# Splitting each run of eight back groups around the last unit of a round in the first feed-forward

## The chip, the cores and the metric

One NeuronCore of a Trainium2 chip runs the whole program. The metric is the time of one execution on the device in microseconds (us); the kernel before takes 2517.07 us, the median of three runs (2516.57 to 2520.61).

## What is computed

Two transformer blocks follow each other on 1024 tokens of width 1024, in float32. The change lies in the feed-forward of the first:

```python
h = rmsnorm(x, norm2_w)
u = causal_dwconv(h @ w_up, ffn_conv_w)          # 3 taps, 2 * 2816 columns
gate, up = u[..., :D_FF], u[..., D_FF:]          # D_FF = 2816 = 22 * 128
x = x + (jax.nn.silu(gate) * up) @ w_down
```

Ahead of it stand a mixer (a gated delta rule and a dilated attention) and its output projection; behind it the second block, with a gated and a convolving branch and a feed-forward of its own. The second block's first part (in2, with a convolution of 31 taps, and out2) is laid into the second half of the first feed-forward.

## The kernel before

**Arithmetic.** A product in float32 is made of three in a rounded format: each weight tile `w` is split into a high part `wh` (ScalarE, line 960) and a low part `wl = w - wh` (VectorE, line 1335), each activation into `hh`/`hl` or `fh`/`fl`, and TensorE adds wh*h, wh*hl and wl*h. Activations lie with channels on partitions and tokens along the free side, and tokens are taken in two halves of 512 (a = 0 and 1).

**Units.** A weight tile of 128 x 1024 numbers (512 KB) is a unit, numbered in order of use. A `gate` or `up` unit is 24 matmuls of 512 columns (lines 2140 to 2142) into one of the banks 0 to 2. Two `down` units are used together as a run of eight groups (lines 2157 to 2159), one group of six matmuls for each 128 rows of x; groups take turns in banks 3, 4 and 5, so that group t needs the bank of group t-3, freed when VectorE has added it into x (line 1638). A matmul starts every 0.227 us, so that a unit is 5.44 us and a group 1.36.

**A round** (`ffn1(a, p)` and `down(1, a, p - 1)`) makes the activations 2p and 2p+1 and projects those of the round before back to 1024 channels: gate A, up A, gate B, up B, then a run of eight groups. There are 11 rounds for each half; the first round of a = 0 has no run, and the run of the last activations of a = 0 stands in the first round of a = 1. After a unit ScalarE evacuates it (1168 and 1170 or 1172, 1175), VectorE makes two passes of the short convolution (1643, 1649). ScalarE takes silu of the gate (1196), VectorE multiplies (`fin`, 1654), ScalarE rounds to fh (1202), VectorE makes fl (`low`, 1658). `fin` and `low` of a pair are put in front of the next gate unit's stage (at a round's end, of the next round's gate A).

**Weights.** There are two raw buffers (unit k uses k % 2) and four slots of wh and wl (k % 4). SyncE's queue loads unit k (line 858) when the low part of unit k-2 is done, or its high part alone where k-2 is "kept". ScalarE's split of unit k waits for that load, and for TensorE to be done with unit k-4. The gate, up and down units of a = 1 are kept, 66 of them: their low parts are those of a = 0, which GpSimd's queue has stored (935), and SyncE's queue brings them back into wl (868) when TensorE is done with unit k-4. The order is load(k), then the bringing back of k-1, on one queue.

**Order.** The class `Dense` writes one list of stages, and every engine and queue walks it in that order, leaving out what is not its own. So an instruction that waits holds back all that is behind it on its engine. A split is put in front of each unit (`prep(at + 3)`), behind group 2 of a run and behind the run. The planner keeps two clocks, `matmul_us` and `vector_us` (5.44 for a unit, 1.36 for a group, 1.28 for VectorE's part of a split, 0.66 for most other passes), and `background` puts norms, gating and the taps of the long convolution in front of a unit or group as long as VectorE's clock plus the item (and, for norms, a reserve of 1.5) does not pass TensorE's. A norm is the items `ax` (VectorE's scaling, 1677, then ScalarE's high part, 1178) and `al` (VectorE's low part, 1611), in the order ax ax al al.

Of the kernel before, what the change touches and what calls it, by code (L numbers as in the profile page):

```python
# [25 lines left out]
KT = D // P  # L26
# [5 lines left out]
FF1 = 2816 // P  # L32
# [11 lines left out]
N_A, N_B, F_A, N_A2, F_B, N_B2, O_A, O_B = 0, 1, 2, 4, 5, 7, 8, 9  # L44
# [44 lines left out]
class Dense:  # L89
# [32 lines left out]

        return self.counts[signal, stage]

    def prep(self, k):


        if k < U_DENSE:
            self.put("high" if k in self.kept else "prep", k)

# [38 lines left out]

    def single(self, stage, late=()):  # L170

        self.prep(self.at + 3)
        for item in late:
            self.put(*item)
        self.matmul_us = max(self.matmul_us, self.vector_us - UNIT_US) + UNIT_US
        self.background(self.matmul_us)
        n = len(self.singles)
        self.tile[stage], self.bank[stage] = self.at, (n % 3, self.singles[n - 3] if n >= 3 else None)
        self.singles.append(stage)
        self.at += 1  # L180
        self.put(*stage)

    def down(self, f, a, p, stats=None):

        self.tile["down", f, a, p] = self.at
        for t in range(KT):
            stage = ("group", f, a, p, t)
            self.matmul_us = max(self.matmul_us, self.vector_us - 2 * GROUP_US) + GROUP_US
            if stats is None:
                self.background(self.matmul_us)  # L190
            n = len(self.groups)
            self.bank[stage] = 3 + n % 3, (self.groups[n - 3] if n >= 3 else None)
            self.groups.append(stage)
            self.put(*stage)
            if t == 2:
                self.prep(self.at + 3)
            if stats is not None:
                for item in self.square(stats, t):
                    self.put(*item)
        if stats is not None:  # L200
            self.put("acc", stats, KT - 2)
            self.put("acc", stats, KT - 1)
        self.at += 2
        self.prep(self.at + 2)

    def square(self, r, k):

# [29 lines left out]
            late = self.square(r, n)  # L237
        return late + [("acc", r, KT - 2), ("acc", r, KT - 1)]

    def ffn1(self, a, p, late=()):  # L240

        for j in (2 * p, 2 * p + 1):
            self.single(("gate", a, j), late)
            self.put("two", a, j)
            self.single(("up", a, j), [("silu", a, j)])
            self.put("two", a, j + FF1)
            self.act[1, a, j] = len(self.act)
            late = [("fin", a, j), ("low", 1, a, j)]
        return late

# [29 lines left out]

    def block_one(self):

        self.prep(self.at + 2)
        late = self.out(1, 0, N_A)
        self.norms += self.factor(N_A) + self.halves(N_A)
        late = self.out(1, 1, N_B, late)
        self.finish(self.norms)
        self.norms += self.factor(N_B) + self.halves(N_B)
        self.reserve = 1.5
        for a in range(2):  # L290
            for p in range(FF1 // 2):
                if (a, p) == (0, 2):
                    self.gating += [("gturn",), "|", "|", ("gbias",)]
                late = self.ffn1(a, p, late)
                if (a, p) == (1, 0):
                    self.reserve = 0.0
                    self.down(1, 0, FF1 // 2 - 1, F_A)
                    self.norms += self.factor(F_A) + self.in_place(F_A) + self.factor(F_A + 1) + self.halves(F_A + 1)
                elif p:
                    self.down(1, a, p - 1)  # L300
                if (a, p) == (1, IN2_AFTER[0]):
                    self.finish(self.norms)
                    late = self.in2(0, late)
                elif (a, p) == (1, OUT2_AFTER[0]):
                    self.drain()
                    late = self.out(2, 0, N_A2, late)
                    self.norms += self.factor(N_A2) + self.halves(N_A2)
        self.finish(self.norms)
        self.block_two(late)

    def block_two(self, late):

        for a in range(2):
            for p in range(FF2 // 2):
                late = self.ffn2(a, p, late)
                if (a, p) == (0, 0):
                    self.down(1, 1, FF1 // 2 - 1, F_B)
                    self.norms += self.factor(F_B) + self.in_place(F_B) + self.factor(F_B + 1) + self.halves(F_B + 1)
                elif (a, p) == (1, 0):
                    self.down(2, 0, FF2 // 2 - 1, O_A)  # L320
                    self.norms += ["|", ("fcols", 0), "|", ("finv", 0)]
                    for t in range(4):
                        self.norms += ["|", ("fturn", 0, t)]
                elif p:
                    if (a, p) == (1, FF2 // 2 - 1):
                        for item in late:
                            self.put(*item)
                    self.down(2, a, p - 1)
                if (a, p) == (0, IN2_AFTER[1]):
                    self.finish(self.norms)  # L330
                    late = self.in2(1, late)
                elif (a, p) == (0, OUT2_AFTER[1]):
                    self.drain()
                    late = self.out(2, 1, N_B2, late)
                    self.norms += self.factor(N_B2) + self.halves(N_B2)
            self.finish(self.norms)
        self.down(2, 1, FF2 // 2 - 1, O_B)
        for item in [("fcols", 1), ("finv", 1)] + [("fturn", 1, t) for t in range(4)]:
            self.put(*item)
# [205 lines left out]
def program(nc, a, out):  # L545

    ctx = ExitStack()
    with ctx:
# [190 lines left out]
        def cols(w, c):  # L739

            return w.rearrange("(k p) n -> p k n", p=P)[:, :, bass.ds(c, P)]

        def rows(w, r):
            return w[bass.ds(r, P), :]
# [15 lines left out]
        dense = Dense(kept)  # L760
# [5 lines left out]
        def _(sp):  # L766
            def load(k, src, m=0, i=0, down=False):

                if k >= 2:
                    sp.wait_ge(s["w_lo"], k - 1 + m * i)  # L770
                dst = raw[:, k % 2] if down else raw[:, k % 2].rearrange("p (k n) -> p k n", k=KT)
                sp.dma_start(dst, src).then_inc(w_loaded[k % 2], 16)
# [94 lines left out]
                        sp.wait_ge(st_free[k % 4], 112 + 16 * sent_before(k))  # L867
                    sp.dma_start(wl[:, k % 4].bitcast(F32), wl_s[:, kept[k]]).then_inc(tile_moved[k % 4], 16)

            for stage in dense.order:  # L870
                if stage[0] == "out":
                    k, n = unit_of[stage], stage[3]
                    if k >= U_OUT1 + 4:
                        load(k, cols(w_out if stage[1] == 1 else w_out2, n * P))
                elif stage[0] == "gate":
                    load(unit_of[stage], cols(w_up, stage[2] * P))
                elif stage[0] == "up":
                    load(unit_of[stage], cols(w_up, (FF1 + stage[2]) * P))
                elif stage[0] == "ffn2":
                    load(unit_of[stage], cols(w_ff1, stage[2] * P))  # L880
                elif stage[0] == "u":
                    load(unit_of[stage], cols(w_in2, stage[2] * P))
                elif stage[0] == "v":
                    load(unit_of[stage], cols(w_in2, (GH + stage[2]) * P))
                elif stage[0] == "val":
                    load(unit_of[stage], cols(w_in2, (2 * GH + stage[2]) * P))
                elif stage[0] == "sig":
                    load(unit_of[stage], cols(w_in2, (3 * GH + stage[2]) * P))
                elif stage[0] == "group" and stage[4] == 0:
                    k, p = unit_of[("down",) + stage[1:4]], stage[3]  # L890
                    for m in range(2):
                        load(k + m, rows(w_down if stage[1] == 1 else w_ff2, (2 * p + m) * P), down=True)
# [59 lines left out]
        def _(act):  # L952
# [45 lines left out]
            square(1)  # L998
            square(2)
            prep(0, 0)  # L1000
            act.wait_ge(s["par_ready"], 1)
            for j in range(4):
                high(j)
            prep(1, 1)
            high(4)
            high(5)
# [21 lines left out]
            for n in range(12):  # L1028
                prep(n + 2, (n + 2) % 4)
                act.wait_ge(s["scaled"], n + 1)  # L1030
                if n >= 4:
                    act.wait_ge(st_free[n % 4], 16 * (n // 4))
                A(st[:, n % 4], acc(n % 2 if n != 2 else 2), ACT.Copy, scale=(0.125 if n < 4 else 1.0)).then_inc(s["st_written"], 1)
# [1242 lines left out]
```

## Time and profile before

| | us |
|---|---|
| median of three runs | 2517.07 |
| lowest, highest | 2516.57, 2520.61 |
| profiled execution | 2516.36 |
| its span (first to last instruction) | 2514.6 |
| TensorE busy in the span | 2465.0 (98%) |
| VectorE busy | 1510.5 (60%) |
| ScalarE busy | 1098.6 (44%) |
| granted TensorE clock | 0.996 of full |

Busy time of TensorE counts the overlapping records of matmuls once. The 16 engines of the DMA moved 304.36 MB, 121 GB/s on average. All durations below come from the profiled execution. Times in it run from the start of the span.

### The profile page before, as it was taken

To read this page: it belongs to the slowest core of one execution; us is meant where nothing else is said; L and a number is where in the kernel's file an instruction comes from. 1 tells how busy PE (TensorE), PEld (TensorE's weight loads), DVE (VectorE), ACT (ScalarE), POOL (GpSimd) and SP (SyncE) were. 2 spreads that over 40 slices of the span, in tenths; PEclk is the share of its full clock that TensorE was granted. 3 is DMA by queue.
4 is the path that set the end of the run, shared out by engine and by line. 5 is a ranking of instruction groups with operands and counts; after the bars stand their busy time and mean duration, and the time that the engine had idled before them with its cause. 6 is when DMAs were issued, how large, how long until landed. Compare 5 with 4: busy or idle time off the path is not lost.

```text
span 2514.6 us, 35248 instructions
## 1 busy us (share of the span) xinstructions
PE 2465.0 (98%) x13947; PEld 2025.6 (81%) x13947; DVE 1510.5 (60%) x2483; ACT 1098.6 (44%) x1783; POOL 55.2 (2%) x110
## 2 busy tenths in 40 slices
PE   7999999999999999999999999999999999999998
PEld 5888777787788888888888788787888888888887
DVE  4234546666366766656669844565888646655555
ACT  4123247776545444446444453444333433433332
POOL 0000000000000011000000000000000000000000
PEclk9999999999999999999999999999999999999999
DMA  6322330110445565565435564423323332333332
GB/s 212 104 84 84 121 118 19 61 61 19 124 122 173 193 201 188 198 209 178 141 93 185 158 193 132 153 84 93 93 84 92 101 99 86 117 106 96 98 88 82
DMA packets 318646, 304.36 MB, mean 121 GB/s; under 512 B 10271, under 2 KB 277908, under 8 KB 318356
## 3 DMA queue, kind: packets, MB, share of 16 engines
q1 hardware_dynamic: 301956, 241.30, 32.4%
q0 software_dynamic: 14400, 56.11, 5.5%
q10 hardware_dynamic: 2128, 4.72, 0.5%
q8 instruction: 111, 1.82, 0.3%
q14 instruction: 51, 0.42, 0.1%
HBM read 244.41 MB, written 57.67 MB: 120 GB/s over the span
## 4 chain that ended last, share of the span: by engine, by line
PE 88%; DVE 6%; ACT 2%; issue 2%; DMA 1%; SPq 0%; DVEq 0%; ACTq 0%
PE PS L2140 15%; PE PS L2142 14%; PE PS L2141 14%; PE PS L1794 11%; PE PS L2157 7%; PE PS L2159 7%; PE PS L2158 7%; PE PS L1965 3%; PE PS L2099 1%; PE PS L1951 1%; PE PS L2075 1%; PE PS L2087 1%; DVE cg L1741 1%; DVE x L1638 1%; DMA raw<-in_w_ff 1%
## 5 line engine op out<-in xcount | busy, mean ns | idle before, releaser
L2140 PE MATMUL PS<-hh,wh 128*128 128x512 f32 x1728 | 677.8, 392 | 2.4 <-DVE hl L1611 1.6
L2142 PE MATMUL PS<-hh,wl 128*128 128x512 f32 x1728 | 673.5, 390 | 0.0
L2141 PE MATMUL PS<-hl,wh 128*128 128x512 f32 x1728 | 673.1, 390 | 0.0
L960 ACT ACTIVATE wh<-raw 128x1024 fp32r<-128x1024 f32 x352 | 366.7, 1055 | 482.5 <-PE PS L2159 343.1
L1335 DVE TENSOR_TENSOR wl<-raw,wh 128x1024 fp32r<-128x1024 f32 x286 | 346.1, 1222 | 280.1 <-ACT wh L960 279.9
L1638 DVE TENSOR_TENSOR x<-x,PS 128x512 f32<-128x512 f32 x432 | 292.6, 683 | 167.3 <-PE PS L2159 166.0
L2140 PEld LDWEIGHTS PS<-hh,wh 128*128 128x128 f32 x1728 | 325.0, 188 | 71.9 <-DVE hl L1611 3.3
L2142 PEld LDWEIGHTS PS<-hh,wl 128*128 128x128 f32 x1728 | 324.8, 188 | 68.0
L2141 PEld LDWEIGHTS PS<-hl,wh 128*128 128x128 f32 x1728 | 325.1, 188 | 66.8 <-issue 0.5
L2157 PE MATMUL PS<-fh,wh 128*128 128x512 f32 x856 | 339.1, 396 | 9.0 <-DVE x L1638 8.9
L2159 PE MATMUL PS<-fh,wl 128*128 128x512 f32 x856 | 334.2, 390 | 0.0
L2158 PE MATMUL PS<-fl,wh 128*128 128x512 f32 x856 | 333.8, 390 | 0.0
L2157 PEld LDWEIGHTS PS<-fh,wh 128*128 128x128 f32 x856 | 161.1, 188 | 47.6 <-DVE x L1638 13.5
L2158 PEld LDWEIGHTS PS<-fl,wh 128*128 128x128 f32 x856 | 161.2, 188 | 34.4 <-issue 1.7
L2159 PEld LDWEIGHTS PS<-fh,wl 128*128 128x128 f32 x856 | 161.0, 188 | 33.9
L1741 DVE SCALAR_TENSOR_TENSOR cg<-cg,par 128x512 f32<-128x512 f32 x240 | 169.7, 745 | 1.3
L1794 PE MATMUL PS<-hh,wh 128*128 128x512 f32 x416 | 129.4, 392 | 0.0
L1794 PE MATMUL PS<-hl,wh 128*128 128x512 f32 x416 | 128.3, 390 | 0.0
L1794 PE MATMUL PS<-hh,wl 128*128 128x512 f32 x416 | 128.1, 389 | 0.0
L1643 DVE SCALAR_TENSOR_TENSOR uc<-ubuf,par,uc 128x512 f32<-128x512 f32 x44 | 33.1, 751 | 107.9 <-ACT uc L1175 107.8
L1168 ACT ACTIVATE ubuf<-PS 128x512 f32<-128x512 f32 x88 | 52.5, 597 | 102.5 <-PE PS L2142 102.4
L1658 DVE TENSOR_TENSOR fl<-uc,fh 128x512 fp32r<-128x512 f32 x107 | 73.5, 687 | 36.7 <-ACT fh L1202 36.7
(302 smaller groups left out, 2567.6 us busy)
## 6 DMA issues: line engine op xcount, KB each, us to landing
raw<-in_w_ff SPq DMA_DIRECT2D x128, 512.0 KB, 4.0
raw<-in_w_up SPq DMA_DIRECT2D x88, 512.0 KB, 4.3
wl_s<-wl POOLq DMA_DIRECT2D x66, 512.0 KB, 5.4
wl<-wl_s SPq DMA_DIRECT2D x66, 512.0 KB, 3.5
raw<-in_w_in SPq DMA_DIRECT2D x59, 512.0 KB, 3.9
raw<-in_w_down SPq DMA_DIRECT2D x44, 512.0 KB, 5.5
raw<-in_w_out SPq DMA_DIRECT2D x32, 512.0 KB, 3.9
qkvz_s<-st POOLq DMA_DIRECT2D x16, 512.0 KB, 2.9
```

The source lines that it names most:

```text
L960: A(whs(slot), raw[:, k % 2], ACT.Copy).then_inc(s["w_hi"], 1)
L1335: TTo(wls(slot), raw[:, k % 2], whs(slot).bitcast(F32), ALU.subtract).then_inc(s["w_lo"], 1)
L1638: TTo(x[:, t, span(a_)], x[:, t, span(a_)], PS[:, bank, :], ALU.add).then_inc(s["x_done"], 1)
L1741: STT(c, cg[:, 2 + q, i:i + HALF], w, c, ALU.mult, ALU.add).then_inc(s["c_tap"], 1)
L1794: last = mm(acc(bank)[:, t * HALF:(t + 1) * HALF], w(slot)[:, cut], h[:, kk, t * HALF:(t + 1) * HALF], start=kk == order[0] and n == 0, st ...
L1965: last = mm(dst(q, h), left(q, h), right(q, h), start=True, stop=True)
L2140: mm(bank, wh[:, k % 4, cut], hh[:, kk, span(a_)], start=kk == 0, stop=False)
L2141: mm(bank, wh[:, k % 4, cut], hl[:, kk, span(a_)], start=False, stop=False)
L2142: last = mm(bank, wl[:, k % 4, cut], hh[:, kk, span(a_)], start=False, stop=kk == KT - 1)
L2157: mm(bank, wh[:, (k + m) % 4, cut], act_tile(True, f), start=m == 0, stop=False)
L2158: mm(bank, wh[:, (k + m) % 4, cut], act_tile(False, f), start=False, stop=False)
L2159: last = mm(bank, wl[:, (k + m) % 4, cut], act_tile(True, f), start=False, stop=m == 1)
```

## The change

In each round that has a run, the fourth unit (up B) is issued between groups 3 and 4 of the run. The four groups ahead of it take the down units' weights before up B is used, but up B keeps the lower unit number: its weights are loaded first, and SyncE's queue now walks a list sorted by unit number. The splits are counted by one running number. One still stands in front of gate A, up A and gate B, none in front of up B; one is put behind group 2, one behind group 6, and one behind the run. Background items may be put in front of each group and of up B as before. The second feed-forward is untouched.

```diff
-    def down(self, f, a, p, stats=None):
-
-        self.tile["down", f, a, p] = self.at
+    def down(self, f, a, p, stats=None, between=None):
+
+        d = self.at + (1 if between else 0)
+        self.tile["down", f, a, p] = d
...
-            if t == 2:
-                self.prep(self.at + 3)
+            if t == 2 or t == 6 and between:
+                self.split()
...
+            if between and t == KT // 2 - 1:
+                self.inner = True
+                between()
+                self.inner = None
...
-        self.at += 2
-        self.prep(self.at + 2)
+        self.at = d + 2
+        self.split()
```

```diff
     def single(self, stage, late=()):
-        self.prep(self.at + 3)
+        if self.split_next <= self.at + 3 and self.inner is None:
+            self.split()
```

```diff
-    def ffn1(self, a, p, late=()):
+    def ffn1(self, a, p, late=(), back=None):
         for j in (2 * p, 2 * p + 1):
+            self.act[1, a, j] = len(self.act)
             self.single(("gate", a, j), late)
             self.put("two", a, j)
-            self.single(("up", a, j), [("silu", a, j)])
-            self.put("two", a, j + FF1)
-            self.act[1, a, j] = len(self.act)
+
+            def up(j=j):
+                self.single(("up", a, j), [("silu", a, j)])
+                self.put("two", a, j + FF1)
+
+            if back and j % 2:
+                self.down(*back, between=up)
+            else:
+                up()
```

```diff
+        self.loads = [("group",) + stage[1:] + (0,) if stage[0] == "down" else stage
+                      for stage, _ in sorted(self.tile.items(), key=lambda item: item[1])]
...
-            for stage in dense.order:
+            for stage in dense.loads:
```

`split()` takes the next number from `split_next` and puts the same stage as `prep(k)` did.

## Rows read from the trace of the kernel before

**Rows 1.** The profile's page: TensorE's busy time, shares of the chain

```profile
PE 2465.0 (98%) x13947; PEld 2025.6 (81%) x13947; DVE 1510.5 (60%) x2483; ACT 1098.6 (44%) x1783; POOL 55.2 (2%) x110
...
PE 88%; DVE 6%; ACT 2%; issue 2%; DMA 1%; SPq 0%; DVEq 0%; ACTq 0%
```

**Rows 2.** Busy time by stretch: stretch, its us, then each engine, clock, DMA

```profile
756.00:1106.00 350.00, 350.00 (x1554) 289.77 (x1553) 229.22 (x296) 152.11 (x252) 32.42 (x61) 1.00 0.57 191
1106.00:1632.00 526.00, 520.49 (x2357) 428.94 (x2356) 335.43 (x493) 249.14 (x385) 1.35 (x3) 1.00 0.50 157
```

**Rows 3.** TensorE's waits from 1106 to 1632: total us, times, longest

```profile
PE PS L2157 <- DVE x L1638: 2.9, 3, 1.7
PE PS L2169 <- ACT cs L1304: 1.5, 2, 0.9
PE PS L2140 <- DVE hl L1611: 1.1, 1, 1.1
```

**Rows 4.** Time line of TensorE: start us, us, engine, line, what

```profile
964.70 0.39 PE L2157 MATMUL PS<-fh,wh 128*128 128x512 f32 x1
...
975.58 0.39 PE L2140 MATMUL PS<-hh,wh 128*128 128x512 f32 x1
...
997.34 0.39 PE L2157 MATMUL PS<-fh,wh 128*128 128x512 f32 x1
```

**Rows 5.** Time line of VectorE in the run from 964.70

```profile
969.58 1.22 DVE L1335 TENSOR_TENSOR wl<-raw,wh 128x1024 fp32r<-128x1024 f32 x1
```

**Rows 6.** Time line of ScalarE in the round from 975.58

```profile
975.84 2.01 ACT L960 ACTIVATE wh<-raw 128x1024 fp32r<-128x1024 f32 x2 [8.75 <-PE PS L2159]
...
981.22 0.60 ACT L1168 ACTIVATE ubuf<-PS 128x512 f32<-128x512 f32 x1 [0.59 <-PE PS L2142]
...
984.13 0.63 ACT L1196 ACTIVATE gc<-gc 128x512 f32<-128x512 f32 x1 [0.32 <-DVE gc L1649]
986.66 0.60 ACT L1168 ACTIVATE ubuf<-PS 128x512 f32<-128x512 f32 x1 [1.90 <-PE PS L2142]
...
991.30 0.63 ACT L1202 ACTIVATE fh<-uc 128x512 fp32r<-128x512 f32 x1 [2.46 <-DVE uc L1654]
992.10 0.60 ACT L1168 ACTIVATE ubuf<-PS 128x512 f32<-128x512 f32 x1 [0.16 <-PE PS L2142]
...
997.54 0.60 ACT L1168 ACTIVATE ubuf<-PS 128x512 f32<-128x512 f32 x1 [1.89 <-PE PS L2142]
```

**Rows 7.** Time line of VectorE in the same round

```profile
977.00 2.36 DVE L1335 TENSOR_TENSOR wl<-raw,wh 128x1024 fp32r<-128x1024 f32 x2 [0.53 <-ACT wh L960]
979.28 0.68 DVE L1654 TENSOR_TENSOR uc<-gc,uc 128x512 f32<-128x512 f32 x1
...
989.45 1.22 DVE L1335 TENSOR_TENSOR wl<-raw,wh 128x1024 fp32r<-128x1024 f32 x1
...
1000.33 1.98 DVE L1638 TENSOR_TENSOR x<-x,PS 128x512 f32<-128x512 f32 x3
```

**Rows 8.** Time line of SyncE's queue: the load behind rows 5

```profile
970.83 0.37 SPq L858 DMA_DIRECT2D raw<-in_w_up  x1
```

**Rows 9.** DMA issues, us to landing: from 970.5; the second of two, from 979.3

```profile
raw<-in_w_up SPq DMA_DIRECT2D x1, 512.0 KB, 4.3
...
raw<-in_w_down SPq DMA_DIRECT2D x1, 512.0 KB, 5.8
```

**Rows 10.** Time line of TensorE: the two long waits for adds into x

```profile
1168.44 0.50 PE L2157 MATMUL PS<-fh,wh 128*128 128x512 f32 x1 [1.67 <-DVE x L1638]
...
1621.26 0.50 PE L2157 MATMUL PS<-fh,wh 128*128 128x512 f32 x1 [1.04 <-DVE x L1638]
```

**Rows 11.** Line 868 from 1106 to 1632, all 64 transfers

```profile
DMA to landing us min/median/max: 3.2/3.5/6.8
```

**Rows 12.** Time line of ScalarE in a round with two ax

```profile
850.66 0.60 ACT L1168 ACTIVATE ubuf<-PS 128x512 f32<-128x512 f32 x1 [0.59 <-PE PS L2142]
...
856.57 0.58 ACT L1168 ACTIVATE ubuf<-PS 128x512 f32<-128x512 f32 x1
```

More of the change, by code:

```diff
@@ L123, in count, with split @@
         return self.counts[signal, stage]
-    def prep(self, k):
+    def split(self):
+        k, self.split_next = self.split_next, self.split_next + 1
         if k < U_DENSE:
@@ L281, in block_one @@
     def block_one(self):
-        self.prep(self.at + 2)
+        self.split_next, self.inner = self.at + 2, None
+        self.split()
         late = self.out(1, 0, N_A)
@@ L293, in block_one @@
                     self.gating += [("gturn",), "|", "|", ("gbias",)]
-                late = self.ffn1(a, p, late)
+                back = (1, 0, FF1 // 2 - 1, F_A) if (a, p) == (1, 0) else (1, a, p - 1) if p else None
                 if (a, p) == (1, 0):
                     self.reserve = 0.0
-                    self.down(1, 0, FF1 // 2 - 1, F_A)
+                late = self.ffn1(a, p, late, back)
+                if (a, p) == (1, 0):
                     self.norms += self.factor(F_A) + self.in_place(F_A) + self.factor(F_A + 1) + self.halves(F_A + 1)
-                elif p:
-                    self.down(1, a, p - 1)
                 if (a, p) == (1, IN2_AFTER[0]):
```

## The prediction

> **What bounds the kernel now.** I read the page's head first. TensorE is busy for 98% of the span and holds 88% of the chain that ended last [rows 1], so only time in which TensorE stands still, or new matmuls, can move the end. The change adds no matmul. Next the view by stretches, cut where the second half of the sequence begins: from 756 to 1106 us TensorE is busy for 350.00 of 350.00 us; from 1106 to 1632 us for 520.49 of 526.00 [rows 2]. The eleven rounds of the first feed-forward on tokens 0 to 511 lie in the first stretch, those on tokens 512 to 1023 in the second. The waits of TensorE in the second are 2.9 us on VectorE's adds into x, 1.5 on ScalarE's cs and 1.1 on hl, together 5.5 us [rows 3]. In the first there are none. That is the ceiling: a pure reordering cannot win more than 5.5 us (0.22%) here, and in the first half it can only lose. About 0.2% (5 us) is what a measurement of this kernel can tell from no change.
>
> Then the time lines of one undisturbed round, from its gate unit at 975.58 to group 0 at 997.34, a run before it from 964.70 [rows 4]. Call 975.58 "zero" of a round: gate A at 0, up A at 5.44, gate B at 10.88, up B at 16.32, groups 21.76 to 32.64, and the next round's gate A at 32.64. Beside it stand VectorE, ScalarE and the loads of the same round [rows 5 to 9]. What the reader is to see: both engines wait for TensorE in each unit, but in a fixed order, so one instruction that waits for a load holds all behind it.
>
> **Part 1, the groups.** Groups 0 to 3 move from 21.76 to 16.32; up B moves to 21.76; groups 4 to 7 stay at 27.20. Group 3 needs the bank of group 0. VectorE adds group 0 only after both passes over the unit before it: ScalarE begins that unit's evacuation at 997.54, VectorE's first add starts at 1000.33 [rows 6, 7], and lasts 0.68, so 3.47 us from evacuation to free bank. Group 3 starts 4.08 us after the unit's end and the evacuation 0.20 after it: 0.4 us of slack. It is now needed after gate B. If the evacuation of gate B is late by more than 0.4 us, group 3 waits for the excess; the wait of 1.67 us at 1168.44 [rows 10], which only such an add ended, shows this very thing, with a first matmul of 0.50 instead of 0.39. I add 0.1 for that.
>
> **Part 2, the weights of the pair of down units.** The second one's slot is freed by up A (10.88) and is now needed at 16.32 instead of 21.76. In the first half VectorE ends that split at 989.45+1.22 = 990.67, which is 15.09 [rows 7]: 1.2 us to spare. In the second half its low part comes by a transfer, issued when gate B starts; over all 64 of the second stretch such a one lands in 3.5 us at the median, 6.8 at the longest [rows 11]. Against 5.44 this holds as a rule, so I cost it nothing, and at most 1.4 us once or twice.
>
> **Part 3, the split that moves.** This is the step that costs. Six splits a round stay, but their places change: the one that stood in front of up B goes behind group 2, and the one behind group 2 goes behind group 6. Name the latter's unit n+7 (n is gate A's number). Unit n+9, the next up B, shares its raw buffer, so the queue of SyncE loads n+9 only when n+7's low part is done. In the trace that low part runs from 969.58 to 970.80 [rows 5] and ends 6.10 us after the run began (964.70); the load is issued at 970.83 and lands 4.3 us later [rows 8, 9]: 0.4 us before the next gate A at 975.58. Moved behind group 6, the chain of the second half-run has the same shape, but starts from up B's end at -5.44: low part done at +0.66, load issued at +0.69, landed at +5.0 to +5.1. The instruction that waits for it, the high part of n+9, stands on ScalarE in front of "fin" and gate A's evacuation; on VectorE its low part stands in front of the product of "fin".
>
> From rows, steady round, first half: high part of n+9 from 5.05; its low part 1.16 later (977.00 less 975.84) for 1.22, done at 7.43; product 0.68, done at 8.03; fh 0.63, done at 8.70; gate A's evacuation at 8.6 (neighbours overlap by 0.1) instead of 5.64 (981.22): 3.0 late. From there to the end of silu is 3.54 (984.13+0.63 less 981.22): up A's evacuation at 12.1, due at 11.08 (986.66): 1.0 late. From there 4.01 to the end of the low part of Part 2: 16.1, needed at 16.32, so it just holds. And 5.27 less 0.1 to the end of fh: gate B's evacuation at 17.3 instead of 16.52, 0.8 late. Less the slack of 0.4, plus 0.1: group 3 waits 0.5 us a round. Up B then lets both engines recover, and the next round loses it again, for the chain starts at up B's end.
>
> Who pays: rounds 2 to 10 of the first half (nine; the first run is in round 1). In the second half most splits have no low part on VectorE and loads go out once the high part is done, which ScalarE does right after up B's evacuation: nothing. Rounds 4 to 10: 7 times 0.5 = 3.5 us. Rounds 2 and 3 carry the norm of the other half as well. By the planner's costs the middle of the run takes four norm items in front of up B (it holds 23.0 of 27.2 us then), so in front of up A stand two "al" and the gate mask in round 2, two "ax" in round 3. Round 2: two "al" of about 0.7 and the mask of about as much (operations of 128x512 on VectorE, as the product at 979.28, 0.68 [rows 7]) behind the low part that ends at 12.6 make up A's first pass 1.1 later: 0.5+1.1 = 1.6. Round 3: with two ax, from gate A's evacuation (850.66) to up A's (856.57) take 5.91 [rows 12], so 8.6+5.9 = 14.5, 3.4 late; less 0.6 of slack along the way, plus 0.1: 2.9. Sum of the first half: 3.5+1.6+2.9 = 8.0 us. Its ends: 0, if some cover that I do not see takes up the 3 us (in the trace gate A's evacuation is never this late, so no row excludes it); and 16, if the loads land 0.9 us later (the second of two loads issued within 1.1 us of each other took 5.8 [rows 9]): 7 times 1.4, and 2.5 and 3.8.
>
> A weighing of the measured load: the row says 4.3 us for 512 KB. The Trainium skill, "DMA: Bandwidth & Descriptors", section "Anatomy of one DMA", gives a fixed 2.0 us and then bytes over 436 GB/s, fitted for DMAs that GpSimd issues; for this load an estimate by that page is 3.2 us. By it gate A's evacuation would be only 1.9 us late, silu would end before up A, steady rounds would lose nothing, and the first half some 2.5 us. The row decides; what the page would have is the second rival's condition. [...]
>
> **Part 4, the second half.** Of the 5.5 us of waits, 2.9 are in runs: one at group 3 with sums beside it (1.67), one at group 6 behind a split (1.04) [rows 10], and one of the rest. Two bursts of four give VectorE 5.44 us of room between them, so a wait at group 6 goes; one at group 3 behind a unit stays likely. The cs and hl waits lie where the planner drops them and may move. Bounds: -5.5, all gone, to +3, three new ones of the size of the 1.04. I take -1.5, half of the 2.9.
>
> **Sum.** Profiled execution: 2516.36 (span 2514.6 and 1.8 around it) + 8.0 - 1.5 = 2522.9. The median of the three runs is 0.7 above it: about 2523.5.
>
> **The rivals.** (A) The cover holds: something in front of the late split gives way and steady rounds lose nothing. For: the slack missed is only 0.4 us a round, the size of one overlap that I read off. Then the first half costs 0 to 4, less 1.5: 2517.5. (B) Faster: the late load costs nothing and the runs of the second half wait no more. Place: the bank waits in front of groups 3 and 6. Price: up to -5.5, so 2511.6. It decides if the load lands within about 3.3 us of its issue, so that gate A's evacuation is under 2 us late, and if cs and hl waits go too. Against: in the first half no row has such a load, and cs and hl are not touched by the split run. (C) The load lands later still, because the pair's next load and two stores of low parts follow at its heels: 5.8 instead of 4.3 [rows 9]. Then gate A is 4.5 late, up A 2.5, the down unit's low part ends at 17.6, and each steady round loses 2.0: 7 times 2.0 + 3.1 + 4.4 - 1.5 = 20 us, 2537; about 2530 if every second load is hit.
>
> **How the numbers follow.** Forecast 0.56 (2519 to 2528), A 0.24, B 0.08, C 0.12. Slower by over 0.2% (above 2522.1): most of the forecast and all of C, 0.60. Within: the forecast's low end and A, 0.33. Faster: B's far end, 0.07. Range: A's low end to C's half case, 2515 to 2531.
>
> **What would show it.** In the first half new waits of TensorE at group 3 on an add into x, nine of them, about 0.5 us each and larger in rounds 2 and 3; ScalarE's splits released by a load into raw (in_w_up) instead of by TensorE; gate A's evacuation 8.6 instead of 5.6 us into a round. If the first half stays at 350 of 350 us busy, Part 3 is wrong. If waits stand at group 0 on the split or on the landing, Part 2 was under-priced. If the second half's waits on x grow, Part 4 has the wrong sign.

## The result, and the profile after

The changed kernel takes 2539.61 us, median of three runs (2536.53 to 2539.79); the kernel before 2517.07. The ratio is 1.0081, interval 1.0061 to 1.0100: 20 us slower (the two medians alone are 22.5 apart). The forecast was slower by 6.5 us, 2523.5, with 2531 as the far end. The sign was right, and the first half of the sequence paid about what was forecast. The size was three times too small, because the second half, which was forecast to win 1.5 us, lost more than the first.

The line numbers of the changed kernel are 16 higher from the splits on: 976 is ScalarE's high part, 1351 VectorE's low part, 1184 to 1191 the evacuation, 1654 the add into x, 874 the load, 2156 to 2158 a unit, 2173 to 2175 a group. In the kernels of the experiments they stand 1 below to 8 above these (980 in e3 is 976 here). The page's head and its chain, as in [rows 1]:

```profile
PE 2474.1 (98%) x13947; PEld 2028.7 (80%) x13947; DVE 1505.8 (59%) x2483; ACT 1096.1 (43%) x1783; POOL 55.4 (2%) x110
...
PE 77%; DVE 10%; ACT 5%; issue 4%; DMA 3%; SPq 0%; DVEq 0%; ACTq 0%
```

TensorE is still busy for 98% of the span. It is the chain that tells: TensorE held 88% of it, now 77%, and VectorE, ScalarE and the DMA have what it lost. Busy time by stretch, as in [rows 2], cut at the same places of the program:

```profile
759.00:1116.00 357.00, 352.82 (x1552) 288.37 (x1552) 226.13 (x296) 149.51 (x251) 32.52 (x61) 1.00 0.57 186
1116.00:1652.00 536.00, 523.30 (x2355) 430.76 (x2354) 332.57 (x492) 248.65 (x384) 1.35 (x3) 0.99 0.49 153
```

The first half has lost its full 350 of 350: 4.2 us idle. The second has 12.7 us idle where it had 5.5, and a clock of 0.99. TensorE's waits of the second half (1120 to 1650), to be held against [rows 3]:

```profile
PE PS L2185 <- ACT cs L1320: 4.2, 2, 3.4
PE PS L2173 <- ACT wh L976: 2.9, 1, 2.9
PE PS L2173 <- DVE x L1654: 2.7, 2, 2.4
PE PS L2156 <- DVE hl L1627: 1.6, 1, 1.6
PE PS L2197 <- DVE small L1686: 0.3, 1, 0.3
```

When the starts of the same units are laid side by side (TensorE's time line, counted in units), the 20.1 us between the two spans fall apart as follows, each line rounded. An idle sum misses part of this. The wait of 0.24 us shown below belongs to a round that lost 0.57: neighbouring matmuls overlap (0.39 long, 0.227 apart), a wait breaks the overlap, and the first matmul behind it takes 0.50. Two longer waits also had a slow clock behind them (last section).

```
                                        us over before
ahead of the first feed-forward               2.5   (same program; 0.6 in a later execution)
tokens 0 to 511, rounds 2 and 3               4.0   (round 2 1.0, round 3 3.0)
                 rounds 4 to 10               3.7   (0.48 to 0.59 each)
                 round 1                     -0.3
tokens 512 to 1023, round 1 (its run)        -1.5
                 round 3                     +5.2
                 rounds 4, 5, 6        +1.9 +4.4 +0.4
                 round 10, and the unit behind it   -1.4 +1.5
```

**The first half as the prediction had it.** ScalarE in the round whose gate unit begins at 983.28, to be held against [rows 6] (start, length, instruction, what ended the wait before it):

```profile
983.54 1.06 ACT L976 ACTIVATE wh<-raw 128x1024 fp32r<-128x1024 f32 x1 [3.31 <-PE PS L2175]
988.42 1.06 ACT L976 ACTIVATE wh<-raw 128x1024 fp32r<-128x1024 f32 x1 [3.82 <-DMA raw<-in_w_up]
991.45 0.63 ACT L1218 ACTIVATE fh<-uc 128x512 fp32r<-128x512 f32 x1 [1.97 <-DVE uc L1670]
991.99 0.58 ACT L1184 ACTIVATE ubuf<-PS 128x512 f32<-128x512 f32 x1
...
995.42 0.58 ACT L1184 ACTIVATE ubuf<-PS 128x512 f32<-128x512 f32 x1
...
1000.59 0.58 ACT L1184 ACTIVATE ubuf<-PS 128x512 f32<-128x512 f32 x1
```

SyncE's queue in the same round, to be held against [rows 8]:

```profile
983.97 0.37 SPq L874 DMA_DIRECT2D raw<-in_w_up  x1
```

TensorE's wait at group 3 of that round:

```profile
1004.11 0.50 PE L2173 MATMUL PS<-fh,wh 128*128 128x512 f32 x1 [0.24 <-DVE x L1654]
```

And VectorE ahead of it, with the low part and the adds into x:

```profile
998.20 1.22 DVE L1351 TENSOR_TENSOR wl<-raw,wh 128x1024 fp32r<-128x1024 f32 x1
...
1003.37 1.88 DVE L1654 TENSOR_TENSOR x<-x,PS 128x512 f32<-128x512 f32 x3
```

The reader is to see one load, issued 0.69 us into the round, and a split that waits 3.82 us for it; fh and the evacuation of gate A follow on its heels, at 8.71 us into the round.

Rounds 2 and 3 pay in another place. TensorE's waits of the first half (756 to 1120), then, from round 3, whose gate unit begins at 848.14, VectorE's low part and the wait of TensorE that it ends:

```profile
PE PS L2173 <- DVE wl L1351: 2.5, 2, 2.2
PE PS L2173 <- DVE x L1654: 1.7, 8, 0.2
...
865.49 1.22 DVE L1351 TENSOR_TENSOR wl<-raw,wh 128x1024 fp32r<-128x1024 f32 x1
866.81 0.47 PE L2173 MATMUL PS<-fh,wh 128*128 128x512 f32 x1 [2.18 <-DVE wl L1351]
```

The eight waits on an add into x are those of group 3 in rounds 3 to 10. The two on wl stand at group 0 of rounds 2 (0.34) and 3 (2.18): the low part of the second down unit is done 18.6 us into round 3, and group 0 needs it at 16.3.

**The second half as it did not.** ScalarE at the end of round 2 and in round 3, whose gate unit begins at 1218.2:

```profile
1216.26 0.63 ACT L1194 ACTIVATE hh<-hn 128x512 fp32r<-128x512 f32 x1 [1.35 <-DVE hn L1693]
1217.53 0.63 ACT L1194 ACTIVATE hh<-hn 128x512 fp32r<-128x512 f32 x1 [0.63 <-DVE hn L1693]
1218.06 1.99 ACT L976 ACTIVATE wh<-raw 128x1024 fp32r<-128x1024 f32 x2
1222.93 1.06 ACT L976 ACTIVATE wh<-raw 128x1024 fp32r<-128x1024 f32 x1 [2.88 <-DMA raw<-in_w_up]
...
1226.53 1.30 ACT L1194 ACTIVATE hh<-hn 128x512 fp32r<-128x512 f32 x2 [2.02 <-DVE hn L1693]
1227.73 0.58 ACT L1184 ACTIVATE ubuf<-PS 128x512 f32<-128x512 f32 x1
...
1235.24 0.58 ACT L1184 ACTIVATE ubuf<-PS 128x512 f32<-128x512 f32 x1
...
1236.38 1.05 ACT L976 ACTIVATE wh<-raw 128x1024 fp32r<-128x1024 f32 x1
```

SyncE's queue there:

```profile
1219.13 0.38 SPq L874 DMA_DIRECT2D raw<-in_w_up  x1
```

The split of n+7 ought to follow up B's evacuation, 5 us before the round. It starts at 1218.06, because two copies of the norm stand ahead of it and each waits for VectorE. So the load goes out 0.9 us into the round, the split of n+9 waits for it, the copies behind it wait in turn, up A's evacuation is 6 us late, and the high part of the second down unit (1236.38) ends at 1237.43, when TensorE has been idle since 1234.7. TensorE's time line there:

```profile
1237.64 0.77 PE L2173 MATMUL PS<-fh,wh 128*128 128x512 f32 x1 [2.93 <-ACT wh L976]
...
1240.34 0.51 PE L2173 MATMUL PS<-fh,wh 128*128 128x512 f32 x1
```

And the stretches of the wait and just behind it. The granted clock is the first of the last three numbers, the DMA's share and its GB/s follow:

```profile
1234.70:1237.60 2.90, 0.01 (x1) 0.00 (x0) 0.97 (x2) 2.73 (x5) 0.00 (x0) 0.92 0.01 3
1237.60:1240.30 2.70, 2.66 (x6) 2.15 (x7) 1.90 (x4) 1.33 (x4) 0.00 (x0) 0.50 0.52 149
```

In round 5 it is the taps. The copies of the convolution's norm (1328, 1194) hold the split of n+7 until 1384.38, the load is issued at 1385.44, and VectorE, whose fl stands ahead of five taps, waits for the high part behind it:

```profile
1386.97 0.69 DVE L1670 TENSOR_TENSOR uc<-gc,uc 128x512 f32<-128x512 f32 x1
1391.02 0.69 DVE L1674 TENSOR_TENSOR fl<-uc,fh 128x512 fp32r<-128x512 f32 x1 [3.36 <-ACT fh L1218]
```

VectorE's 3.4 us of standing still are not made good, since the planner has filled it up to TensorE's clock, and TensorE pays them 19 us later, in front of the norm's sums, where the kernel before waits 0.65:

```profile
1409.90 1.05 PE L2185 MATMUL PS<-ones,cs 128*128 128x1 f32 x8 [3.42 <-ACT cs L1320]
```

### The profile page after: what moved, and what is told of

It reads as the page before. It is cut to its first block, busy times and chain, and to the rows that moved or that the text cites. A ratio compares the mean times of both kernels' runs of the same rounds, so it can differ in the third digit from the quotient of the medians.

```text
span 2534.7 us, 35248 instructions
## 1 busy us (share of the span) xinstructions
PE 2474.1 (98%) x13947; PEld 2028.7 (80%) x13947; DVE 1505.8 (59%) x2483; ACT 1096.1 (43%) x1783; POOL 55.4 (2%) x110
## 4 chain that ended last, share of the span: by engine, by line
PE 77%; DVE 10%; ACT 5%; issue 4%; DMA 3%; SPq 0%; DVEq 0%; ACTq 0%
PE PS L2156 12%; PE PS L2157 12%; PE PS L2158 12%; PE PS L1810 11%; PE PS L2173 6%; PE PS L2175 5%; PE PS L2174 5%; PE PS L1981 3%; DMA raw<-in_w_up 2%; DVE x L1654 2%; DVE cg L1757 2%; DVE wl L1351 1%; PE PS L2115 1%; PE PS L1967 1%; PE PS L2091 1%
```

## The experiments

All kernels below are timed against the kernel before on their own chip; times in brackets are medians there. Before had 2519.42 beside e1 to e4, 2518.74 beside e5 to e8, 2518.93 beside e9.

**Theory L (late load).** The split that moved behind group 6 makes the load of unit n+9 late; the loss is in what stands behind that load's split in the fixed orders of ScalarE and VectorE. **Rival S (short room).** Group 3's bank and the second down unit's weights are needed one unit sooner, and that costs wherever the split stands.

**e1, e2: one half alone.** In `ffn1`, with `a == 1` for the second:

```diff
-            if back and j % 2:
+            if back and j % 2 and a == 0:
                 self.down(*back, between=up)
             else:
                 up()
+                if back and j % 2:
+                    self.down(*back)
```

> The changed order in the rounds of tokens 0 to 511 alone (rounds 1 to 10); the rounds of tokens 512 to 1023 as before the change. If the two halves lose independently, as the comparison of the two traces says (7.3 us between the first gate of round 0 and the first gate of the second half, 10.4 behind it), this kernel takes 7.3 us more than before: about 2524.5, ratio 1.003. If the loss of the second half is inherited from a delay of the first, it takes nearly the whole 20 us more: 2537.

> The changed order in the rounds of tokens 512 to 1023 alone. Independent halves: 10.4 us more than before, about 2527.5, ratio 1.004, with the large waits of TensorE again in rounds 3, 4 and 5 of that half. Inherited from the first half: under 3 us more, 2520 or less.

Measured: e1 1.0029 (1.0018 to 1.0040), 2527.17; e2 1.0051 (1.0036 to 1.0066), 2532.00. The halves lose independently: 7.7 and 12.6 us by the medians, together 20.3. In e1's trace no round of the second half is more than 0.03 us longer or shorter than before; in e2's round 3 is 6.1 and round 5 6.0 us longer than before. So most of the loss was where the prediction had put a gain. e1 came out as expected; e2 lost 2 us more than the 10.4 that I had named.

**e3: fin and low ahead of the late split.** Only the order of three stages in front of gate A (and of other first units of a pair) changes:

```diff
+        if late and late[0][0] == "fin" and not stage[-1] % 2:
+            for item in late:
+                self.put(*item)
+            late = ()
         if self.split_next <= self.at + 3 and self.inner is None:
             self.split()
```

> The changed kernel, except that in front of gate A the stages fin and low of the last pair stand ahead of the split of unit n+9 instead of behind it. Nothing is loaded or split sooner. Late load theory (the moved split makes the load of n+9 late, and the loss comes from what stands behind its split in the queues of ScalarE and VectorE): the product, fh and fl no longer wait, gate A's evacuation is 0.5 us late instead of 3.0, steady rounds of the first half lose 0 instead of 0.5, round 3 loses about 0.5 instead of 3; second half at most 3 us instead of 10. In all 1 to 6 us more than before: 2518 to 2523. Rival, short room (group 3 and the second down unit's weights are needed one unit sooner, and that costs by itself, wherever the split stands): within 4 us of the changed kernel, 2534 or more.

Measured: 1.0005 (0.9995 to 1.0014), 2520.45 against 2519.42. No load goes out sooner and no deadline has moved back, yet 19 of 20 us are gone by the ratios. The loads of rounds 3 and 5 of the second half are issued 0.9 and 0.4 us into the round, as in the changed kernel, and the second half as a whole loses 0.5 us in this trace instead of 10.4. Rival S, which wanted 2534 or more, is out as the main cause. ScalarE in the round from 977.45:

```profile
980.73 0.63 ACT L1222 ACTIVATE fh<-uc 128x512 fp32r<-128x512 f32 x1 [1.96 <-DVE uc L1674]
982.41 1.06 ACT L980 ACTIVATE wh<-raw 128x1024 fp32r<-128x1024 f32 x1 [1.05 <-DMA raw<-in_w_up]
983.38 0.58 ACT L1188 ACTIVATE ubuf<-PS 128x512 f32<-128x512 f32 x1
```

The split still waits for its load until 5.0 us into the round, but fh is done by then, and gate A's evacuation is at 5.93 instead of 8.71. Rounds 4 to 10 cost nothing; round 3 0.8; in the second half round 3 still costs 2.5.

**e4: the moved split alone.** The unit order of before, one number changed for the first feed-forward's runs:

```diff
-            if t == 2 or t == 6 and between:
+            if t == (6 if f == 1 and (a, p) != (1, FF1 // 2 - 1) else 2):
```

> The kernel before with one thing of the change: in the runs of the first feed-forward the split behind group 2 stands behind group 6. The order of units and groups on TensorE is as before. Late load theory: the load of n+9 lands about 5 us into the next round, gate A's evacuation there is 3.0 us late; in the first half the run's groups come a unit later, so that TensorE does not wait: 0 to 2 us; in the second half, where VectorE is filled with taps up to TensorE's clock, part of the 10 us: 2 to 8 us. In all 2519 to 2526. Short room theory: no difference, 2516.5 to 2518, since no deadline has moved.

Measured: 1.0011 (1.0001 to 1.0020), 2521.92 against 2519.42. The split's move costs by itself, 2.5 us. Its waits of TensorE in the first half, where before has none:

```profile
PE PS L2172 <- DVE x L1653: 2.9, 3, 1.1
```

The trace has gate A's evacuation as late as the changed kernel has (988.64 in the round from 979.91). But group 3 then comes one unit later, and only rounds 2 to 4, in which copies of the norm stand in front of up A, fail to make it good: 1.4 us each, which is more than the 0 to 2 us that I had named for the first half. I had put more into the second half, 2 to 8 us; there it costs 1.6 in round 6 and wins 1.4 in round 10. The 1.6 are not waits: TensorE's waits in that round are those of before (0.15 and 0.88), but behind them the granted clock is 0.50 from 1443.1 to 1446.3, where before it is 1.00. So neither is enough alone, by the medians: the late split costs 2.5 with the old deadlines, the early deadlines about 1 when fin and low no longer stand behind the waiting split (e3), the two together 20.

**e5, e6: the split behind group 4, without and with e3's edit.**

```diff
-            if t == 2 or t == 6 and between:
+            if t == 2 or t == 4 and between:
```

> The changed kernel, except that the late split stands behind group 4 instead of group 6; fin and low stay behind the split of n+9. Late load theory: the low part of n+7 is done 1.3 us sooner in the first half (VectorE needs 1.22 for it and 0.68 for each add, and it no longer waits for group 6), the load lands 3.8 us into the round instead of 5.05, gate A's evacuation is 1.8 late instead of 3.0, silu ends before up A does, steady rounds lose 0, rounds 2 and 3 together 2 instead of 4; in the second half the split stands ahead of the background copies in front of groups 5 and 6, and at most half of the 10 us is left. In all 2 to 6 us more than before, and 12 to 18 less than the changed kernel. Short room theory: as the changed kernel, 20 us more than before.

> Both mends together: split behind group 4, and fin and low ahead of the split of n+9. Late load theory: first half within 1 us of before; second half better than with fin first alone, since nothing is held; against before from -3 to +1 us. If the split run brings VectorE room where it counts (the waits on x behind L1654), this is the kernel that shows it, and it is faster than before by 1 to 3 us. Short room theory: 15 us or more above before.

Measured: e5 1.0008 (0.9999 to 1.0017), 2521.04; e6 0.9991 (0.9982 to 1.0000), 2516.75; before 2518.74. Against the changed kernel beside them (e8, 2536.72) two groups sooner are worth 16 us. e5 leaves fin, low and every background item where the changed kernel has them, but its split stands ahead of the copies in front of groups 5 and 6. So its loads go out in time in the second half too; in round 3, from 1213.41, the load is issued 3.9 us ahead of the round:

```profile
1209.48 0.38 SPq L874 DMA_DIRECT2D raw<-in_w_up  x1
```

In e5's trace the second half is 1.6 us shorter than before, in e6's 1.7, where the changed kernel's is 10.4 longer. Round 5 costs 0.1 instead of 4.4, and round 3 costs 1.7 in e5 and 1.3 in e6 instead of 5.2. With both edits, the first half is full again:

```profile
756.00:1106.00 350.00, 350.00 (x1554) 289.64 (x1553) 225.47 (x294) 151.87 (x251) 32.95 (x62) 1.00 0.60 191
```

**e7: both mends, and the split run only in rounds 1 and 10 of tokens 512 to 1023.** e1's edit with `(a, p) in ((1, 1), (1, 10))`, e5's, and e3's for the unit behind such a run.

> The split run with both mends in two rounds alone, 1 and 10 of tokens 512 to 1023, where the changed kernel's trace shows 1.5 and 1.4 us won against before (waits in front of group 3 with sums beside it, and of group 6 behind a split); all else as before the change. If these gains belong to the split run itself and not to a delay brought from elsewhere: 1.5 to 3 us less than before, ratio 0.999. If the 1.5 us that the changed kernel pays in front of the second unit of the second feed-forward comes with it: 0 to 1.5 less.

Measured: 0.9987 (0.9978 to 0.9996), 2516.09 against 2518.74: faster than before by 2.6 us, and the only kernel whose interval lies wholly below 1. Its trace wins 2.0 us in round 1 and 1.4 in round 10, and pays 0.7 in front of the second unit of the second feed-forward. The wait of 1.67 at group 3 and that of 1.04 at group 6 [rows 10] are gone; what is left of the adds into x is:

```profile
PE PS L2181 <- DVE x L1662: 0.2, 1, 0.2
```

**e8: the changed kernel again.**

> The changed kernel itself, unaltered, beside the others. Both theories: 18 to 22 us more than before, ratio 1.007 to 1.009. The 2.4 us that its first trace was behind before the first feed-forward had begun, where the two programs are the same, are of that execution: expected under 1 us in this one.

Measured: 1.0074 (1.0059 to 1.0089), 2536.72, 18.0 us more than before and so at the low edge of what I had named. Its trace has 0.3 us over before at the start of the first block's projection and 0.6 at that of the first feed-forward; the 2.5 us of the first trace belong to that execution. The 5.3 us of round 3 and the 4.3 of round 5 of the second half are there again; round 3 of the first half costs 4.0 instead of 3.0.

**e9: the second half without background items in front of groups 5 to 7.** e2's edit and

```diff
-            if stats is None:
+            if stats is None and not (between and t in (4, 5, 6)):
                 self.background(self.matmul_us)
```

> The changed order in the rounds of tokens 512 to 1023 alone, as in e2, and the planner puts no background items in front of groups 5, 6 and 7 of a run (numbers 4, 5 and 6 counted from 0); the split stays behind the group numbered 6, fin and low stay behind the split of n+9. e2 lost 12 us by its two medians. Theory: ScalarE's high part of n+7 is late in this half because copies of the norm and of the convolution (lines 1194, 1257, 1328) stand ahead of it in ScalarE's order and wait for VectorE; without them it follows up B's evacuation, the load of n+9 goes out 3 us before the round begins instead of 0.4 to 0.9 into it, and rounds 3 and 5 lose no 5 and 4 us: -2 to +4 us against before. Rival: the copies have no part in it, the second half loses because two bursts of groups leave VectorE, filled with taps, less room: 8 to 14 us more than before, as e2.

Measured: 1.0017 (1.0007 to 1.0026), 2523.66 against 2518.93: 4.7 us more than before where e2 had 12.6: 0.7 over the -2 to +4 of the theory and far under the 8 to 14 of the rival. With no copy ahead of it, the split of n+7 comes in time: the load of round 3 is issued at 1204.61, about 3.8 us ahead of the round, and round 5 costs nothing. Round 3 still costs 6.1:

```profile
1233.17 0.50 PE L2175 MATMUL PS<-fh,wh 128*128 128x512 f32 x1 [4.08 <-DVE x L1656]
```

The items of the norm that may not stand in the run now stand in front of gate A, up A and gate B, and its copies hold gate B's evacuation until 1229.62, 4.8 us after gate B's end at 1224.85; group 3, due at 1228.9, waits. Here rival S has its part: the room behind gate B is short, and a round full of norm items pays for it. But e9 has changed where these items stand; in e5, which has not, the same round costs 1.7.

## Why the prediction was wrong, step by step

- **Bound and ceiling.** Right: the loss is waits of TensorE, with the slow clock behind some of them, and no kernel came near the 5.5 us that a reordering could win. The best won 2.6.
- **Parts 1 and 3, first half.** Right in mechanism and size for rounds 4 to 10: gate A's evacuation 8.7 us into the round (said 8.6), up A's 12.1 (12.1), the down unit's low part done 16.1 (16.1), gate B's evacuation 17.3 (17.3), seven rounds paying 0.48 to 0.59 us each (0.5), at group 3. e3 and e5 show that the loss hangs on the split that waits for a late load. Round 2 cost 1.0 (1.6) and round 3 3.0 (2.9; 4.0 and 4.1 in e8 and e1), but not where the prediction put it, so that the near match of round 3 is luck. All rounds together cost 7.3 us (8.0), 0.3 of it won in round 1.
- **Part 2.** Right that the weights hold in a steady round (16.1 us, needed at 16.32). Priced at nothing elsewhere, and that failed twice. In rounds 2 and 3 of the first half TensorE waited 0.34 and 2.18 us at group 0 for the second down unit's low part. The prediction's own numbers give this: up A's evacuation at 14.5 in round 3, plus 4.01, is 18.5, 2.2 us past 16.32; I had worked that step out for the steady round alone and put the whole lateness on group 3, which waited 0.24. In round 3 of the second half group 0 waited 2.9 us for a high part; there I had looked at the transfer of the low part alone.
- **Part 3, second half. This step failed, and it decides the result.** It says of the second half that loads go out once the high part is done, "which ScalarE does right after up B's evacuation: nothing". ScalarE's order has background copies between the two. I had used that order for the first half, and for the place of the items in front of up A, and not for the run. In rounds 2, 3, 5 and 6 the load goes out 0.4 to 0.9 us into the round. e5 puts the split ahead of the last copies, the same loads go out 3.0 to 3.9 us ahead of the round, and the second half's +10.4 becomes -1.6. The term was +0 and is about +12. e9, which takes the copies away instead, says the same more roughly, since it also moves the norm's items: 12.6 us become 4.7.
- **Part 4.** -1.5 for the second half, with +3 as the far end; measured +10.4 in the first trace, but -1.6 in e5 and -1.7 in e6, where the loads are in time. So what it is about, the room for VectorE, was sized well, though by halving a sum: the wait at group 3 in round 1, which was to stay likely, went (-1.5), the one at group 6 in round 10 went (-1.4), and 1.5 came back in front of the second unit of the second feed-forward. With Part 3's missing term the sum has the other sign. The bound "three new ones of the size of the 1.04" was drawn from waits of a kernel in which no queue was held, and bounded nothing.
- **The rivals.** The steady rounds did lose, so A's cover was not there. C's 2537 is near the measured time for another reason than C's: the loads landed 4.4 us after their issue and not 5.8, and steady rounds lost 0.5 and not 2.0. The first half of B's condition came true in e6: with the late load no longer in the way, the first half loses nothing. Its 5.5 us did not.
- **The estimate of the load.** An estimate by the Trainium skill ("DMA: Bandwidth & Descriptors", section "Anatomy of one DMA") is 3.2 us. The trace differs, with about 4.4: issued at 983.97, the split that waited for it began at 988.42. The measurement decides; by the prediction's working the steady rounds would have lost nothing with 3.2, and they lost 0.5.

Of round 3 of the second half, about 3.5 of the 5.2 us belong to the late load and 1.7 to the short room: e5 leaves 1.7, with a wait of 1.34 at group 3. The 1.9 us of round 4 of the second half stand in e2, e3, e5, e6 and e9 alike. They are not lateness in the main: TensorE waits 0.73 there for cs, and eight small matmuls of the convolution's norm (line 2197, 1380.01), which held up the next matmul by 0.9, stand in round 4, where the kernel before has them in round 5 (1375.02). Each such set of eight has moved up a round, so that round 6 is without one, and the 1.9 come back there in e3, e5, e6 and e9. This is read from the traces; no kernel tried it. What stays open is which of ScalarE and VectorE decides the loss of a late load in the second half: e3 and e5 relieve both.

## What to carry to other kernels

When a step is moved later, follow what its end releases (here the buffer, then a load of 4.4 us, then a split) and then everything that stands behind the receiver in each engine's fixed order; do it anew for every stretch whose background differs. Here a split's wait of 3.8 us cost 0.5 where the engines had slack, and one of 3.4 cost 4.4, later and elsewhere, where a planner had filled VectorE. Putting work whose input is there ahead of work that waits for a load was worth 17 to 19 us for three swapped stages. And work a late case through every deadline of the steady case again, not only through the one that was tight there.

## What the runs showed of the hardware

After the wait of 2.93 us TensorE came back at half its clock: granted 0.50 (1.2 GHz) from 1237.60 to 1240.30, matmuls 0.43 us apart instead of 0.227, for six matmuls, then 2.4 GHz again. The Trainium skill ("TensorE: Matmul & The Clock Gate", section "HAM oscillation — how this bites in real kernels") warns that a wait for a transfer between bursts of matmuls can bring the clock down; by the granted 0.50 behind this wait the trace agrees.

The length of the wait alone does not decide it. e8 is the same program. Its wait in the same place is 3.05 us and the clock stays at 1.00, while it falls in round 3 of the first half behind a wait of 2.12, where the first trace has 2.18 and 1.00 behind it:

```profile
1235.90 0.47 PE L2173 MATMUL PS<-fh,wh 128*128 128x512 f32 x1 [3.05 <-ACT wh L976]
...
1235.90:1240.30 4.40, 4.36 (x18) 3.27 (x18) 3.60 (x6) 2.73 (x5) 0.00 (x0) 1.00 0.46 123
...
866.00:869.30 3.30, 3.30 (x10) 2.52 (x8) 2.76 (x5) 2.55 (x5) 0.00 (x0) 0.50 0.92 286
```

What it costs differs too. In round 3 of the first half it makes 4.0 us (e8) of 3.0. In round 3 of the second half the six slow matmuls take 1.2 us more, but group 3 then waits 0.28 us instead of the 1.61 of e8, and the round costs 5.2 us with the fall and 5.3 without it. Behind the wait of 3.42 in round 5 the clock is 0.50 from 1411.3 to 1414.6; the waits there have grown by 2.8 us, so that about 1.6 of the round's 4.4 are an estimate of what the clock cost. After the waits of 1.67 us [rows 10] and 0.24 the clock stayed at 1.00, each with a first matmul of 0.50.
